# Second block: probabilities turned by VectorE and 16 transfers, a group's score and value products gathered

## The reference, cut to what matters

```python
h = jnp.einsum('bsd,dc->bsc', x, w_in)
qa, ka, va, za, qb, kb, vb, zb, f_logit, g_logit = jnp.split(h, SPLIT_POINTS, axis=-1)
...
out_a = dilated_mixture(qa, ka, heads(va, N_HEADS_A)).reshape(B, S, WIDTH_A)
up_a = jnp.einsum('bsw,wd->bsd', out_a * jax.nn.silu(za), w_up_a)
log_f = jax.nn.log_sigmoid((f_logit + b_forget).astype(jnp.float32))
out_b = forgetting_attention(heads(qb, N_HEADS_B), heads(kb, N_HEADS_B),
                             heads(vb, N_HEADS_B), log_f).reshape(B, S, WIDTH_B)
up_b = jnp.einsum('bsw,wd->bsd', out_b * jax.nn.silu(zb), w_up_b)
gates = jax.nn.sigmoid(g_logit + b_gate)
g_a, g_b = gates[..., :D_MODEL], gates[..., D_MODEL:]
y = jnp.einsum('bsd,de->bse', g_a * up_a + g_b * up_b, w_out)
return layer_norm(DEEPNORM_ALPHA * x + y, ln_g, ln_b)
```

## Time and profile before

| | us |
|---|---|
| median of three runs | 2801.43 |
| the profiled execution | 2799.75 |
| its span, first to last instruction | 2798.0 |
| PE busy | 2757.6 (99%) |
| PE weight loads (beside its products) | 2253.2 (81%) |
| DVE busy | 1817.0 (65%) |
| ACT busy | 1346.3 (48%) |
| POOL busy | 370.9 (13%) |
| mean granted TensorE clock | 0.994 of full |

### The profile page before, as it was taken

How to read it: one execution, slowest core, us unless ns; L and a number is a source line. 1 busy time by engine, 2 the same in 40 slices (tenths; PEclk the granted TensorE clock), 3 DMA queues, 4 the chain that set the end, 5 groups by cost and what they waited for, 6 DMA issues and landing times.

```text
span 2798.0 us, 35964 instructions
## 1 busy us (share of the span) xinstructions
PE 2757.6 (99%) x13157; PEld 2253.2 (81%) x13157; DVE 1817.0 (65%) x2220; ACT 1346.3 (48%) x1765; POOL 370.9 (13%) x653
## 2 busy tenths in 40 slices
PE   8899999999999999999999999999999999999998
PEld 5477887888888888888888888888888888888886
DVE  7889899778657556655555556575565545555565
ACT  3255646556544453544444544444445444445443
POOL 0000010000001223100133100022131011331000
PEclk9999999999999999999999999999999999999999
DMA  9987798865655566566566566565566665665554
GB/s 397 414 311 241 272 342 307 309 222 190 215 194 181 188 201 205 185 220 196 191 202 203 191 196 223 181 195 187 191 203 205 208 199 183 206 206 187 193 213 148
DMA packets 178617, 622.74 MB, mean 223 GB/s; under 512 B 27688, under 2 KB 27984, under 8 KB 173088
## 3 DMA queue, kind: packets, MB, share of 16 engines
q1 hardware_dynamic: 155376, 583.08, 60.3%
q0 software_dynamic: 23088, 37.56, 4.6%
HBM read 599.51 MB, written 2.14 MB: 215 GB/s over the span
## 4 chain that ended last, share of the span: by engine, by line
PE 90%; DMA 4%; DVE 4%; ACT 1%; issue 0%; SPq 0%; DVEq 0%; ACTq 0%
PE acc L860 65%; PE acc L2455 16%; DMA raw<-in_w 2%; DVE wlo L1865 1%; PE psS L839 1%; PE psS L829 1%; DMA scr<-in_w_early 1%; PE psS L2455 1%; PE psS L2421 1%; PE psT L812 1%; PE psT L2378 1%; DMA mraw<-in_w_early 1%; DVE raw L1900 0%; PE psS L2440 0%; PE psT L2340 0%
## 5 line engine op out<-in xcount | busy, mean ns | idle before, releaser
L489 DVE TENSOR_TENSOR wlo<-raw,whi 128x1024 fp32r<-128x1024 f32 x670 | 819.4, 1224 | 783.7 <-ACT whi L372 782.0
L372 ACT ACTIVATE whi<-raw 128x1024 fp32r<-128x1024 f32 x670 | 708.9, 1059 | 980.3 <-PE acc L860 964.4
L860 PE MATMUL acc<-whi,tokens_hi 128*128 128x512 f32 x2304 | 632.3, 395 | 0.5 <-DVE tokens_lo L303 0.3
L860 PE MATMUL acc<-whi,tokens_lo 128*128 128x512 f32 x2304 | 618.2, 389 | 0.0
L860 PE MATMUL acc<-wlo,tokens_hi 128*128 128x512 f32 x2304 | 618.1, 389 | 0.0
L860 PEld LDWEIGHTS acc<-whi,tokens_lo 128*128 128x128 f32 x2304 | 432.4, 188 | 91.5
L860 PEld LDWEIGHTS acc<-wlo,tokens_hi 128*128 128x128 f32 x2304 | 432.4, 188 | 91.0
L860 PEld LDWEIGHTS acc<-whi,tokens_hi 128*128 128x128 f32 x2304 | 425.7, 188 | 85.6 <-DVE tokens_lo L303 0.9
L1564 ACT ACTIVATE whi<-raw 128x1024 fp32r<-128x1024 f32 x160 | 168.7, 1058 | 200.8 <-PE acc L2455 116.2
L1865 DVE TENSOR_TENSOR wlo<-raw,whi 128x1024 fp32r<-128x1024 f32 x160 | 195.3, 1223 | 82.2 <-ACT whi L1564 81.3
L2455 PE MATMUL acc<-whi,tokens_hi 128*128 128x512 f32 x800 | 226.1, 403 | 1.9 <-DVE tokens_lo L1974 1.2
(11 more groups left out here) (355 smaller groups left out, 2434.2 us busy)
## 6 DMA issues: line engine op xcount, KB each, us to landing
raw<-in_w SPq DMA_DIRECT2D x838, 512.0 KB, 4.2
raw<-in_w_late SPq DMA_DIRECT2D x80, 512.0 KB, 5.0
mraw<-in_w SPq DMA_DIRECT2D x64, 512.0 KB, 4.7
mraw<-in_w_late SPq DMA_DIRECT2D x48, 512.0 KB, 4.8
y<-in_w_early SPq DMA_DIRECT2D x12, 1024.0 KB, 15.4
mraw<-in_w_early SPq DMA_DIRECT2D x7, 1024.0 KB, 14.9
scr<-in_w_early SPq DMA_DIRECT2D x7, 1024.0 KB, 14.8
sgl<-in_w_early SPq DMA_DIRECT2D x6, 1024.0 KB, 15.0
```

Of the source, the lines that this page charges most:

```text
L372: act.activation(whi[:, n % SLOTS, :], raw[:, n % SLOTS, :], ACT.Copy).then_inc(s_hi, 1)
L489: dve.tensor_tensor(wlo[:, n % SLOTS, :], raw[:, n % SLOTS, :], whi[:, n % SLOTS, :].bitcast(F32), ALU.subtract).then_inc(s_lo, 1)
L860: m = pe.matmul(acc[c % 2][:, tb, :], a[:, kk, tb * P:(tb + 1) * P], b[:, n % SLOTS, k * CW:(k + 1) * CW], start=(kk == 0 and q == 0), sto ...
```

## The change

The 12 identity products of a group (line 812) and the three ACT copies (line 392) go. In their place, at the new step r = 34 (`R_PROB`), DVE turns all three units of `prob` at once in 32x32 blocks (128 partitions x 1536) into `pb`, and POOL moves the blocks to `probT` by 16 DMAs, as it does for q and k. A DMA moves 32 partitions x 12 x 32 elements, against 32 x 8 x 32 for q and k. `pb` lies in the memory of `qT` and `kT`, which are now one tile, `qkT`: their data are dead after the scores. POOL's q DMAs of the next group therefore wait for the 16 DMAs of this group's probabilities (`s_pT`).

All three score units now stand at r = 26, before one granule. The third one goes to the PSUM bank `psT`, which the identity products used. Both value units stand at r = 37, before one granule, and wait there for the 16 new DMAs. DVE's two output steps move from r = 40, 41 to r = 41, 42, and the turn of the gated result from r = 42 to r = 43.

```diff
 R_SCORES = 26
-R_BLOCKS = R_SCORES + 16
+R_PROB = R_SCORES + 8
+R_BLOCKS = R_SCORES + 17
...
+MOVED = 16 * QUADS * QUADS
...
-        if 0 <= r - R_SCORES - 5 <= 2:
-            out += [("p", grp, r - R_SCORES - 5)]
+        if r == R_SCORES:
+            out += [("s", grp, 2)]
...
-        if 0 <= r - R_SCORES <= 2:
-            out += [("s", grp, r - R_SCORES)]
-        if 0 <= r - R_SCORES - 10 <= 1:
-            out += [("o", grp, r - R_SCORES - 10)]
+        if r == R_SCORES:
+            out += [("s", grp, 0), ("s", grp, 1)]
+        if r == R_SCORES + 11:
+            out += [("o", grp, 0), ("o", grp, 1)]
...
+    pb = qkT[:].rearrange("p h t -> p (h t)")[:, 0:3 * CW]
...
             for i, (dst, signal) in enumerate(((qT, s_qT), (kT, s_kT))):
-                pool.wait_ge(s_blk, 3 * n + i + 1)
-                if grp:
-                    pool.wait_ge(*unit_full(l, ("s", grp - 1, 2)))
-                elif l:
-                    pool.wait_ge(*unit_full(l - 1, ("s", NGRP - 1, 2)))
+                pool.wait_ge(s_blk, 4 * n + i + 1)
+                if n:
+                    pool.wait_ge(s_pT, MOVED * n)
...
+            blocks_moved(probT[:].rearrange("p u (k t) -> p (u k) t", t=P), pb.rearrange("p (k t) -> p k t", t=P), s_pT)
+            pool.wait_ge(s_blk, 4 * n + 4)
             blocks_moved(zT, zb, s_zT)
...
-                    fill_copy(("p", grp, u), probT[:, u, :])
...
+                if r == R_PROB:
+                    dve.wait_ge(s_exp, at(l, 3 * NGRP, 3 * grp + 3))
+                    dve.transpose(pb, prob[:].rearrange("p u n -> p (u n)")).then_inc(s_blk, 1)
...
-                if 0 <= r - R_SCORES - 14 <= 1:
+                if 0 <= r - R_SCORES - 15 <= 1:
...
-                    for k in range(4):
-                        t = pe.transpose(bank[:, k * P:(k + 1) * P], prob[:, name[2], k * P:(k + 1) * P], ident[:])
+                    t = scores(name, bank)
...
-                    for p in ((0,), (1, 2))[tb]:
-                        pe.wait_ge(*copied(l, ("p", grp, p)))
+                        pe.wait_ge(s_pT, MOVED * (NGRP * l + grp + 1))
```

More of the change, by code:

```diff
@@ L171, in second_block @@
     stage = sb("stage", [P, TB, CW])
-    qT = sb("qT", [P, HPG, SEQ])
-    kT = sb("kT", [P, HPG, SEQ])
+    qkT = sb("qkT", [P, 2 * HPG, SEQ])
+    qT, kT = qkT[:, 0:HPG, :], qkT[:, HPG:, :]
     v = sb("v", [P, TB, CW])
@@ L216, in second_block @@
     s_kT = sem("c_kT")
+    s_pT = sem("c_pT")
     s_zT = sem("c_zT")
@@ L420, in attention @@
                     evacuate(c0 + 2, v, ACT.Copy)
[L421 to L424, removed]
-                    fill_copy(("p", grp, u), probT[:, u, :])
                 if r == R_SCORES + 12:
                     if NGRP * l + grp:
-                        act.wait_ge(s_blk, 3 * (NGRP * l + grp))
+                        act.wait_ge(s_blk, 4 * (NGRP * l + grp))
                     evacuate(c0 + 3, z, ACT.Silu)
@@ L582, in rope @@
                     if which:
[L583 to L584 removed]
+                        dve.wait_ge(s_blk, 4 * n + 1)
+                        dve.wait_ge(s_qT, MOVED * (n + 1))
                     elif n:
[L586 removed]
+                        dve.wait_ge(s_blk, 4 * n - 2)
                 half = HD // 2
@@ L628, in attention @@
                     name = ("s", grp, u)
-                    bank = UNIT2[name] % 2
+                    if u < 2:
+                        bank, full, free = psS[UNIT2[name] % 2], unit_full(l, name), s_sfree[UNIT2[name] % 2]
+                        read = unit_read(l, name)
+                    else:
+                        bank, full, free = bank_t(name), filled(l, name), s_tfree[FILL2[name] % 2]
+                        read = copied(l, name)
                     n, w = (HPG, P) if u == 0 else (2, SEQ)
@@ L637, in attention @@
                             dve.wait_ge(s_cmask, l + 1)
-                    dve.wait_ge(*unit_full(l, name))
+                    dve.wait_ge(*full)
                     if u == 0 and NGRP * l + grp:
-                        dve.wait_ge(s_zT, 16 * QUADS * QUADS * (NGRP * l + grp))
+                        dve.wait_ge(s_zT, MOVED * (NGRP * l + grp))
                     p = prob[:, u, :].rearrange("p (h s) -> p h s", s=w)
-                    dve.tensor_tensor(p, psS[bank][:].rearrange("p (h s) -> p h s", s=w), m, ALU.add)\
-                        .then_inc(s_sfree[bank], 1)
-                    dve.wait_ge(*unit_read(l, name))
+                    dve.tensor_tensor(p, bank[:].rearrange("p (h s) -> p h s", s=w), m, ALU.add).then_inc(free, 1)
+                    dve.wait_ge(*read)
                     if grp >= 3 and u == 0:
@@ L781, in tensor, with scores @@
         for l in range(DEPTH):
+            def scores(name, bank):
+                _, grp, u = name
+                pe.wait_ge(s_qT, MOVED * (NGRP * l + grp + 1))
+                pe.wait_ge(s_kT, MOVED * (NGRP * l + grp + 1))
+                w, tb = (P, 0) if u == 0 else (SEQ, 1)
+                for b in range(CW // w):
+                    h = b + max(0, 2 * (u - 1))
+                    m = pe.matmul(bank[:, b * w:(b + 1) * w], qT[:, h, tb * P:(tb + 1) * P], kT[:, h, 0:w],
+                                  start=True, stop=True)
+                return m
             def fill(name):
@@ L820, in unit @@
                 if name[0] == "s":
[L821 to L829, removed]
+                    m = scores(name, bank)
                 elif name[0] == "o":
```

23 lines of the change are left out of this document (9 added, 14 removed).

## The result

The changed kernel takes 2868.78 us (median of four runs, 2866.63 to 2870.94) against 2800.90 for the kernel before on the same chip: ratio 1.0243, 95% interval 1.023 to 1.0256. It is 68 us slower. The direction was forecast, the size was not: the forecast was +30 us, with a range of 2796 to 2862 us.

A forecast was written before the change was run, and what follows sets the result against it. PE was taken to bound the kernel: −17.5 us of identity products, +12 x 2.5 of waits and +17 of clock gave +29.5 on 2799.75, so 2829.3, or 2831 as median of runs; range 2796 to 2862 us.

The forecast's parts named there:

- PE bounds the second block: Second block: PE busy for all 100 us of a typical stretch; removing the identity products gives back 17.5 us.
- Gathering is worth 0: Score and value products on PE: gathering them saves no entry fee, 0 with a bound of 0.1 us per group.
- The walk to POOL's start: Chain through ACT and DVE to POOL's first new DMA: turn of 1.77 us, POOL starting at T + 22.5.
- T: Start of a group's scores on PE, from which the forecast measured its times; 921.72 in the profile before.
- POOL's pace: POOL issuing the 16 new DMAs: 0.60 us each, bounds 0.574 and 0.86, last issue at T + 31.5.
- The last landing: Last new DMA of a group: probabilities ready at T + 35.2, bounds T + 33.1 and T + 41.0.
- step 5: Landing after the last DMA's issue: 3.5 us plus 0.2 for the waiter; earlier landings took 1.8 to 5.4.
- the last rival: POOL or DMA engines: size counts in full, wait 6.4 us per group, 2881 us, or 2856 at half; chance 0.17.
- the flat slope of the POOL instruction: POOL's issue: 0.491 us for 16 rows, 0.584 for 256 pieces, so 0.63 for 384 pieces on that slope.
- When PE wants them: Value products on PE, behind scores and granules 26 to 36: wanted at T + 32.7, so PE waits 2.5 us per group.
- The clock: PE after each wait: clock falls to 1.2 GHz in 10 of 12 groups, 1.7 us each, 17 us in all.
- The rest costs nothing: POOL's gated-result and q sets and DVE's output steps, up to one granule (2.72 us) later: cost nothing, hidden by POOL's list.

The follow-up runs named there:

- E5: Changed kernel with the block turn at step 33, value products at step 39, output steps and gated-result turn together at step 42: 2781.2 us, ratio 0.9928.
- E9: E5 with the block turn left at step 34, value products at step 39 and outputs together at step 42: 2783.5 us, ratio 0.9937.
- E2: Kernel before with only the gathering of score units and value products, identity products and ACT's copies kept: 2799.1 us, ratio 0.9996.
- E4: Changed kernel loading only the first half of every weight granule of the second block, 256 KB instead of 512 KB: 2798.4 us in one run.
- E8: Changed kernel with the 16 DMAs moving only two of three units of the probabilities, 32 KB each: 2825.2 us, ratio 1.0091.
- E7: Changed kernel with the 16 DMAs of the probabilities issued by ACT at its step 35 instead of by POOL: 2864.4 us, ratio 1.0229.
- E3: Changed kernel with 36 unread identity products on PE before the wait for the probabilities: 2843.6 us, ratio 1.0159.
- E6: Changed kernel with only the block turn moved, to step 33 instead of 34: 2827.8 us, ratio 1.0092.
- E1: Changed kernel with value products, output steps, gated-result turn and split three granules later, forget-gate products and their steps five later: 2837.1 us, ratio 1.0135.

## Why the prediction missed the size, point by point

- *PE bounds the second block; its products cost what they cost.* Right. The 17.5 us are seen in E5 and E9.
- *Gathering is worth 0.* Right, shown by E2.
- *The walk to POOL's start.* Forecast T + 22.5; measured 941.80 − 919.48 = 22.3. The turn: forecast 1.77 us, measured 1.77.
- *POOL's pace.* Forecast 0.60 us per DMA, measured 9.72 / 16 = 0.61; last issue T + 31.4 against 31.5.
- *The last landing.* **This is the step that failed**: "I take 3.5 plus 0.2 for the waiter" (step 5). Measured 5.0 to 7.0 over the 12 groups, 6.2 on average, 6.34 + 0.14 in the first. The 3.5 is just what the last DMA of a set of 32 KB took before (mean of 36 sets), so half as much data again beside the weights was put at nothing. The mechanism was named (DMA engines at 0.86 beside the weights), and a full price stood as a bound and in the last rival; but against it I set the flat slope of the POOL instruction, which is the issue and not the transfer. With the larger transfers the engines are at 0.91 in the issues' stretch and about 1 after it, and the landing goes on growing, from 4.4 us at the fourth DMA to 6.2 at the last, about 0.15 us each. E4 and E8 show both conditions: with fewer weights, or smaller transfers, the climb is gone. The term: 12 x 2.5 = 30 us forecast, 60.9 measured. Open is whether the engines' rate alone sets it or also the way in which POOL's queue shares them (E7).
- *When PE wants them.* Forecast T + 32.7, measured 957.38 − 5.18 − 919.48 = 32.7.
- *The clock.* The mechanism was right; forecast 17 us, measured 24.2, because the longer waits made all 12 fall and each cost 2.0 and not 1.7. E3 shows the cause. At waits near the forecast ones (2.8 us), E6 measures 7 falls in 12, where I had said 10: that share was a guess from four idles.
- *The rest costs nothing.* Right for the change itself: POOL's gated-result and q sets ran into each other, and only one wait of 0.7 us, of DVE, followed. E1 shows how thin that cover was.
- *Rivals.* What happened is the last rival, given 0.17, between its half price (2856) and its full one (2881), through the landing and not through POOL's pace.

The rule of the Trainium skill that I weighed ("DMA: Bandwidth & Descriptors", Anatomy of one DMA — SWDGE path: about 2.0 us plus bytes by 436 GB/s) gives 2.1 us for these transfers. The trace agrees for the first of a set (1.9 to 2.8) and nearly for the last ones of E4 (2.1 to 2.8), and is three times that for the last ones beside the full weight stream. The Trainium skill's rule against the change ("VectorE: DVE Perf Modes", The three transpose paths, and Rules for kernel authors) is to turn 128x128 on TensorE where the result may go to PSUM. E5 does not bear it out for this kernel, in which TensorE is the bound: turning on VectorE and moving by DMA beats the identity products, by 20.5 us, once nobody waits for the landing.

## What to carry to other kernels

When a consumer is moved behind a set of DMAs, add up the load of the DMA engines during the set, not only the length of the issuing instructions: here, at a DMA share of 0.86, sets of 32 KB transfers landed at a level pace, and at 0.91 to 1 those of 48 KB landed later and later along the set. Then place the consumer by the landing of the last transfer, and leave the producer of the next set in the same queue where it was. A wait on TensorE cost about 1.4 times its length here (60.9 + 24.2 us for 60.9), because the clock fell behind it. At 2.1 to 3.7 us of idleness it fell in some groups and not in others, and the runs do not show what decides it.

## What the runs showed of the hardware

- The last of the same 16 DMAs of 48 KB lands after 2.3 us on average when the neighbouring stream moves 256 KB per granule (E4), after 6.2 when it moves 512 KB. Issued by ACT, while the weight stream comes to a stop, it lands after 2.0 (E7).
- The granted clock fell after idles as short as 2.12 us and stayed up after one of 3.21 (E6). Filling most of the idle time with products that nobody reads kept it at full and saved 25 us (E3).
- Issuing a DMA of 32 x 12 x 32 elements takes ACT 0.68 us on average (E7), POOL 0.61.
- The products at the lower clock: 24 printed ones take up to 5.11 us to the next granule, against 2.60 (E5) to 2.71 (E3) at full clock.
